# A two-block transformer kernel: gathers and weights fetched one stage ahead, one root for two norms, and new orders at the openings of four stages

## What is computed

```python
# x: 1024 tokens x 1024 columns, float32; EPS 1e-6
x = x + concat(differential_attention, latent_attention)(rms(x) @ w_in) @ w_out     # first mixer
x = x + cross_attention(rms(x), rms(mem))                                           # 256 memory rows
logits = rms(x) @ routers                       # 4 groups x 8 experts, 2 experts for each token
order = argsort(expert_ids); dest = padded_start[sorted_e] + rank   # 47 blocks of 128 slots, one expert each
y = (silu(h[tok] @ w_gate[e]) * (h[tok] @ w_up[e])) @ w_down[e]     # for each block
x = x + sum of its two rows of y, each times its routing weight
x = rms(x) * norm_final_g                       # end of the first block
h = rms(x) * attn_norm_2                        # start of the second block
proj = h @ w_in_2                               # fox, conv, mlstm and sliding-window mixers, gates
x = x + merge(...) @ w_merge_out; x = x + swiglu(rms(x))
```

## Time and profile before

| what | value |
|---|---|
| median of 3 runs (lowest, highest) | 3330.19 us (3329.55, 3349.68) |
| the profiled execution's own time | 3333.73 us |
| its span | 3332.0 us |
| its mean granted TensorE clock | 0.965 of full speed |
| PE busy, share of the span | 3121.0 us, 94% |
| PEld | 2479.6 us, 74% |
| DVE | 1697.6 us, 51% |
| ACT | 1456.4 us, 44% |
| POOL | 326.4 us, 10% |
| DMA | 413.50 MB, mean 124 GB/s |

### The profile page before, as it was taken

The page is one execution under the profiler, slowest core; times in us unless marked ns, Lnnn a source line. Parts: engine busy times, 40 slices in busy tenths (PEclk is TensorE's granted clock), DMA queues, the critical chain, the costliest instruction groups (busy, mean ns, idle before and its releaser), DMA issues. The chain is left out here.

```text
span 3332.0 us, 39537 instructions
## 1 busy us (share of the span) xinstructions
PE 3121.0 (94%) x14936; PEld 2479.6 (74%) x14936; DVE 1697.6 (51%) x2533; ACT 1456.4 (44%) x2355; POOL 326.4 (10%) x343
## 2 busy tenths in 40 slices
PE   7998999898879999969998999999989989999999
PEld 5766998776757767757776877777777868888787
DVE  4436887424655665562321222332247486666675
ACT  4325787533436666653522333333353342322343
POOL 0001110000212222120000000000000022222000
PEclk9999999999979999979999999999999999999999
DMA  2344221211157777661233222232254323334653
GB/s 96 84 127 120 58 62 40 100 74 49 77 206 273 289 289 277 225 202 45 82 97 105 64 64 76 64 108 83 79 187 160 102 79 111 95 104 131 218 151 112
DMA packets 251533, 413.50 MB, mean 124 GB/s; under 512 B 44999, under 2 KB 159758, under 8 KB 239058
## 3 DMA queue, kind: packets, MB, share of 16 engines
q1 hardware_dynamic: 226706, 365.31, 34.1%
q10 hardware_dynamic: 9088, 28.84, 2.2%
q0 software_dynamic: 15552, 16.82, 1.7%
HBM read 370.01 MB, written 104.30 MB: 142 GB/s over the span
## 5 line engine op out<-in xcount | busy, mean ns | idle before, releaser
L2753 DVE TENSOR_TENSOR moe_wgu_low<-moe_raw,moe_wgu_high 128x2048 fp32r<-128x2048 f32 x92 | 206.7, 2289 | 180.2 <-ACT moe_wgu_high L2711 180.2
L213 PE MATMUL ga_gate<-second_h_high,ga_ws_high 128*128 128x512 f32 x512 | 231.8, 453 | 0.0
L214 PE MATMUL ga_gate<-second_h_low,ga_ws_high 128*128 128x512 f32 x512 | 204.5, 399 | 0.0
L215 PE MATMUL ga_gate<-second_h_high,ga_ws_low 128*128 128x512 f32 x512 | 204.4, 399 | 0.0
L2679 PE MATMUL moe_down<-moe_raw_down,moe_ht 128*128 128x512 f32 x376 | 169.2, 593 | 1.7 <-ACT moe_ht L2743 1.7
L2711 ACT ACTIVATE moe_wgu_high<-moe_raw 128x2048 fp32r<-128x2048 f32 x92 | 170.7, 1906 | 0.0
L3730 ACT ACTIVATE ga_row<-ga_turned 128x256 f32<-128x256 f32 (+4 forms) x96 | 44.7, 465 | 275.3 <-PE ga_turned L3644 275.3
L213 PE MATMUL pr_acc<-second_h_high,pr_ws_high 128*128 128x512 f32 x352 | 147.0, 418 | 11.7 <-DVE pr_stage L3053 8.2
L213 PE MATMUL moe_up<-moe_wgu_high,moe_xt_high 128*128 128x512 f32 x376 | 152.2, 405 | 4.2 <-DVE moe_xt_low L2759 4.2
L213 PE MATMUL up_bank<-second_h_high,up_w_high 128*128 128x512 f32 x352 | 138.3, 393 | 10.8 <-DVE up_w_low L3301 7.7
L215 PE MATMUL moe_up<-moe_wgu_high,moe_xt_low 128*128 128x512 f32 x376 | 148.2, 394 | 0.0
(11 more groups left out here) (592 smaller groups left out, 7961.2 us busy)
## 6 DMA issues: line engine op xcount, KB each, us to landing
moe_raw<-in_w_expert_gate_dram SPq DMA_DIRECT2D x32, 1024.0 KB, 8.4
moe_raw<-in_w_expert_up_dram SPq DMA_DIRECT2D x32, 1024.0 KB, 10.1
moe_raw_down<-in_w_expert_down_dram SPq DMA_DIRECT2D x32, 1024.0 KB, 7.5
scratch_expert_rows<-moe_y ACTq DMA_DIRECT2D x47, 512.0 KB, 8.3
scratch_hidden<-X SPq DMA_DIRECT2D x77, 256.0 KB, 2.1
down_rows<-scratch_hidden SPq DMA_DIRECT2D x73, 256.0 KB, 2.8
ga_w<-in_w_in_dram SPq DMA_DIRECT2D x32, 512.0 KB, 4.2
scratch_gates<-ga_stage SPq DMA_DIRECT2D x64, 256.0 KB, 3.6
```

Of the source, the lines that this page charges most:

```text
L213: nc.tensor.matmul(out, w[0], x[0], start=start, stop=False)
L214: nc.tensor.matmul(out, w[0], x[1], start=False, stop=False)
L215: return nc.tensor.matmul(out, w[1], x[0], start=False, stop=stop)
L2753: nc.vector.tensor_tensor(wgu[i % 2][1][:, :, m, :], raw[(2 * i + m) % RAW][:].rearrange("p (c n) -> p c n", n=FF), wgu[i % 2][0][:, :, m, ...
```

## The change

In `first_tokens` seven raw weight buffers replace six and loads wait only for a buffer; x tile 2 goes ahead of weight chunk 7; a one-element square root (`probe`) loads the root table at the start; root and scale of tile 0 move ahead of weights; and tile 0's product is made in three passes over the chunks: high x high, then activation high x weight low, then activation low x weight high (before: three matmuls chunk by chunk). `mixed_queries` gets the same probe and three passes, and its first splits are reordered. `route` keeps counts by one scan and float32r matmuls, makes the one-hot lanes in two DVE instructions, puts the token numbers on the block side (eight ACT copies), and holds back `first_low` until POOL has issued its two gathers. At the end of `run_experts` SP fetches the next stage's first four weight chunks and the gain, the last result is copied and stored in two halves by ACT and DVE, and POOL gathers tile 0's expert rows there. In `mixer_tokens` a new step `grow` writes x * gain into the first gathered row's buffer `rows[0]`; its square gives the second norm, one root and one reciprocal serve both norms, `scale_rows` and `final_rows` read that buffer, and `final_rows(t - 1)` now comes after `add_experts(t)`, `grow(t)` and `apply_gain(t - 1)`; POOL's gathers for tile t wait for `final_rows(t - 2)` and `scale_rows(t - 2)` as well. The diff, cut to its core and moved left by eight columns:

```diff
     def load_weight(c):
-        if c >= 4:
-            sp.wait_ge(w_highs, c - 3)
-        if c >= 6:
-            sp.wait_ge(w_lows, c - 5)
-        sp.dma_start(raw[c % 6][:], w_view[:, c, COL_VD:COL_CQ]).then_inc(w_in[c % 4], 16)
+        if c >= RING:
+            sp.wait_ge(w_lows, c - RING + 1)
+        sp.dma_start(raw[c % RING][:], w_view[:, c, COL_VD:COL_CQ]).then_inc(w_in[c % RING], 16)
-    for c in range(3, KD):
+    for c in range(3, RING):
         load_weight(c)
     load_x(2)
+    for c in range(RING, KD):
+        load_weight(c)
     load_x(3)
...
+    def first_products():
+        pe.wait_ge(highs, 1)
+        for h_part, w_part in ((0, 0), (0, 1), (1, 0)):
+            if h_part:
+                pe.wait_ge(lows, 1)
+                turn_rows(2)
+            for c in range(KD):
+                if w_part:
+                    pe.wait_ge(w_lows, c + 1)
+                elif not h_part:
+                    pe.wait_ge(w_highs, c + 1)
+                last = nc.tensor.matmul(acc[0][:], H[h_part][:, c, 0:P], w[w_part][:, c, :],
+                                        start=(h_part + w_part + c == 0), stop=(h_part == 1 and c == KD - 1))
+            if h_part + w_part == 0:
+                turn_rows(1)
+        last.then_inc(products, 1)
+
...
     act.dma_start(gain_rows[0:first_count, :], gain_source("norm_mix_g")).then_inc(gain_in, 16)
+    act.wait_ge(k.chains["pool"].sem, 3)
+    nc.scalar.activation(probe[:], k.ones[:, 0:1], ACT.Sqrt)
     square(0)
     weight(0)
+    take_root(0)
+    scale_rows(0)
     weight(1)
-    take_root(0)
     weight(2)
-    scale_rows(0)
     square(1)
+    weight(3)
+    high_part(0)
     take_root(1)
     scale_rows(1)
-    high_part(0)
...
     average(0)
     weight(0)
+    inverse(0)
     weight(1)
-    inverse(0)
+    dve.wait_ge(gains_copied, 1)
+    apply_gain(0)
     weight(2)
     average(1)
+    weight(3)
     inverse(1)
-    dve.wait_ge(gains_copied, 1)
-    apply_gain(0)
     low_part(0)
...
+    def first_out_rows():
+        pe.wait_ge(highs_in, 1)
+        for in_part, w_part in ((0, 0), (0, 1), (1, 0)):
+            if in_part:
+                pe.wait_ge(lows_in, 1)
+                turn_in(1)
+            for c in range(KD):
+                if w_part:
+                    pe.wait_ge(w_lows, c + 1)
+                elif not in_part:
+                    pe.wait_ge(w_highs, c + 1)
+                for h in range(2):
+                    last = nc.tensor.matmul(acc[:, h * HALF:(h + 1) * HALF], inner[0][in_part][:, c, :],
+                                            W[w_part][:, c, h * HALF:(h + 1) * HALF],
+                                            start=(in_part + w_part + c == 0), stop=(in_part == 1 and c == KD - 1))
+        last.then_inc(products, 1)
     turn_in(0)
-    for i in range(ST + 2):
+    first_out_rows()
+    for i in range(1, ST + 2):
...
 
+    nc.scalar.activation(probe[:], k.ones[:, 0:1], ACT.Sqrt)
     squares(0)
-    weight(0)
     root(0)
     latent_scale(0)
+    weight(0)
     weight(1)
+    high_in(0)
     weight(2)
-    high_in(0)
     weight(3)
     squares(1)
+    root(1)
     weight(4)
+    latent_scale(1)
     weight(5)
-    root(1)
-    latent_scale(1)
...
     sums(0)
+    diff_scale(0)
     weight(0)
-    diff_scale(0)
     weight(1)
+    low_in(0)
     weight(2)
-    low_in(0)
+    sums(1)
     weight(3)
-    sums(1)
+    diff_scale(1)
     weight(4)
     weight(5)
-    diff_scale(1)
...
-    link(v.tensor_tensor(both[:, :, :], hot[0][:, :, :], hot[1][:, :, :], ALU.add))
-    link(v.memset(before[:, 0, :], 0.0))
-    for t in range(ST):
-        link(v.tensor_tensor(before[:, t + 1, :], before[:, t, :], both[:, t, :], ALU.add))
-    dve.sem_inc(hot_made, 1)
+    link(v.tensor_tensor(both[:, :, :].rearrange("p e t -> p t e"), hot[:, 0, :, :], hot[:, 1, :, :], ALU.add))
+    dve.wait_ge(made, 15)
+    v.tensor_tensor_scan(upto[:, :, :].rearrange("p e t -> p (e t)"), carried[:, :, :].rearrange("p e t -> p (e t)"),
+                         both[:, :, :].bitcast(F32).rearrange("p e t -> p (e t)"), 0.0, ALU.mult, ALU.add).then_inc(hot_made, 1)
...
-        link(v.tensor_tensor(hot[c][:, :, :], hot[c][:, :, :], place[:, :, :], ALU.mult))
-        link(v.tensor_reduce(slot_f[:, c * ST:(c + 1) * ST], hot[c][:, :, :], AX, ALU.add))
+    link(v.tensor_tensor(placed[:, :, :, :], hot[:, :, :, :], place[:, :, :].rearrange("p (o t) e -> p o t e", o=1)
+                         .broadcast_to([P, 2, ST, E]), ALU.mult))
+    link(v.tensor_reduce(slot_f[:].rearrange("p (c t) -> p c t", c=2), placed[:, :, :, :], AX, ALU.add))
...
+    v.tensor_tensor(hot_block[:, :, :], along(base_f[:], N_BLOCKS),
+                    bases[:, :].rearrange("p (o b) -> p o b", o=1).broadcast_to([P, 2 * ST, N_BLOCKS]),
+                    ALU.is_equal).then_inc(blocks_made, 1)
...
-    for j in range(2 * ST):
-        t = j % ST
-        v.tensor_scalar(hot_lane[j][:], lanes[:], lane_f[:, j:j + 1], tokens[:, t:t + 1],
-                        ALU.is_equal, ALU.mult).then_inc(lanes_made, 1)
+    for c in range(2):
+        v.tensor_tensor(hot_lane[:, c * ST:(c + 1) * ST, :], along(lane_f[:, c * ST:(c + 1) * ST], P),
+                        lanes[:, :].rearrange("p (o n) -> p o n", o=1).broadcast_to([P, ST, P]),
+                        ALU.is_equal).then_inc(lanes_made, 1)
...
+    dve.wait_ge(tabled, 1)
+    link(v.tensor_scalar(empty[:], table[:, 0:N_BLOCKS], 0.0, NO_TOKEN, ALU.is_equal, ALU.mult))
+    v.scalar_tensor_tensor(slot_of_block[:], table[:, 0:N_BLOCKS], -1.0, empty[:], ALU.add, ALU.add).then_inc(slotted, 1)
+    dve.wait_ge(gathers, 1)
     first_low(0)
-    dve.wait_ge(tabled, 1)
-    link(v.tensor_scalar(empty[:], table[:], 0.0, NO_TOKEN, ALU.is_equal, ALU.mult))
-    v.scalar_tensor_tensor(slot_of_block[:], table[:], -1.0, empty[:], ALU.add, ALU.add).then_inc(slotted, 1)
     first_low(1)
...
-    nc.tensor.matmul(counts[:, :], k.ones[:], before[:, ST, :], start=True, stop=True)
-    nc.tensor.matmul(ranks[:, :, :], earlier[:], both[:, :, :], start=True, stop=False)
-    nc.tensor.matmul(ranks[:, :, :], k.ones[:], before[:, 0:ST, :], start=False, stop=True).then_inc(ranked, 1)
+    nc.tensor.matmul(counts[:, :], ones_r[:], upto[:, :, ST - 1], start=True, stop=True)
+    nc.tensor.matmul(ranks[:, :, :], not_earlier_r[:], by_tile[0], start=True, stop=False)
+    nc.tensor.matmul(ranks[:, :, :], ones_r[:], by_tile[1], start=False, stop=True).then_inc(ranked, 1)
     for j in range(2 * ST):
-        pe.wait_ge(lanes_made, j + 1)
-        last = nc.tensor.matmul(table[:], hot_lane[j][:], hot_block[:, j, :], start=(j == 0),
+        pe.wait_ge(tokens_made, j % ST + 1)
+        pe.wait_ge(lanes_made, j // ST + 1)
+        last = nc.tensor.matmul(table[:], hot_lane[:, j, :], token_block[:, j, :], start=(j == 0),
...
+    gain, mixer_raw, _ = ahead
+    sp.wait_ge(ups, N - 1)
+    for c in range(1, 4):
+        load_mixer_weight(k, sp, mixer_raw[c], c)
+    sp.wait_ge(ups, N)
+    sp.dma_start(gain, k.dram["norm_final_g"].rearrange("(o d) -> o d", o=1).broadcast_to([P, D])).then_inc(k.final_gain_in, 16)
+    load_mixer_weight(k, sp, mixer_raw[0], 0)
+    sp.wait_ge(tail_copied, 1)
+    sp.dma_start(y_out[SEQUENCE[N - 1]][:, HALF:], y[(N - 1) % 2][:, HALF:]).then_inc(tail_stored, 16)
...
+    pool.wait_ge(ups, N)
+    pool.wait_ge(stored0, 16 * ((N + 1) // 2))
+    pool.wait_ge(stored1, 16 * (N // 2))
+    pool.wait_ge(tail_stored, 16)
+    for c in range(2):
+        gather_outputs(k, slots, c, 0, ahead[2][c])
...
-        nc.scalar.activation(y[i % 2][:], down[:], ACT.Copy).then_inc(y_ready, 1)
+        cols = slice(0, D if i + 1 < N else HALF)
+        nc.scalar.activation(y[i % 2][:, cols], down[:, cols], ACT.Copy).then_inc(y_ready, 1)
         act.wait_ge(y_ready, i + 1)
-        act.dma_start(y_out[SEQUENCE[i]], y[i % 2][:]).then_inc(stored[i % 2], 16)
+        act.dma_start(y_out[SEQUENCE[i]][:, cols], y[i % 2][:, cols]).then_inc(stored[i % 2], 16)
...
+    dve.wait_ge(downs, N)
+    dve.wait_ge(stored[(N - 1) % 2], 16 * ((N - 1) // 2))
+    nc.vector.tensor_copy(y[(N - 1) % 2][:, HALF:], down[:, HALF:]).then_inc(tail_copied, 1)
...
         if t >= 2:
             pool.wait_ge(added, 2 * (t - 2) + 2)
+            pool.wait_ge(normed, t - 1)
+            pool.wait_ge(scales, t - 1)
         for c in range(2):
-            nc.gpsimd.indirect_dma_start(out=rows[c][t % 2], out_offset=None, in_=k.scratch["expert_rows"],
-                                         in_offset=bass.IndirectOffsetOnAxis(ap=slots[c][:, t:t + 1], axis=0)
-                                         ).then_inc(gathered[t % 4], 16)
+            if t:
+                gather_outputs(k, slots, c, t, rows[c][t % 2])
...
-    weight(0)
-    weight(1)
+    for c in range(4):
+        weight(c)
+    nc.scalar.activation(probe[:], k.ones[:, 0:1], ACT.Sqrt)
     square(0, 0)
-    weight(2)
-    take_root(0, 0)
-    weight(3)
     square(0, 1)
-    take_root(0, 1)
+    take_roots(0)
...
```

(98 more changed lines are left out.)

159 lines of the change are left out of this document (76 added, 83 removed).

## The result

The changed kernel takes 3354.05 us (median of 12 runs, 3350.95 to 3366.46), the kernel before 3330.48 in the same session: a ratio of 1.0075, 95% interval 1.0061 to 1.0089. The forecast was 3351, range 3336 to 3364. The profiled execution took 3354.84 us with a span of 3353.0, the old one's was 3332.0: +21.0. The table puts that together from the two traces; each entry is how far the changed kernel is ahead (-) or behind (+), and how much each part added.

A forecast was written before the change was run, and what follows sets the result against it. PE was taken to bound the kernel, losing time at stage openings, until waits through a shared buffer bound `mixer_tokens`. -7 + 3 - 5.3 + 30.4 = +21 us gave 3354.8 from the profiled run, 3351 from the median; range 3336 to 3364.

The forecast's parts named there:

- First stage, -7: First stage: earlier root, high-part start and earlier tile 1 bring its transposes forward; -7.4, cut to -7 us for gaps.
- the end that I had given as -8.5: First stage: the forecast's fast end, -8.5 us, if the clock rises as soon as tile 0's second pass begins.
- Attention output stage, +3: `mixed_queries`: the late last weight chunk delays second pass, second transposes and add into x; +1.8 to +5.2, taken as +3 us.
- Routing, -5.3: Routing: slots at 927.4 instead of 933.6, first expert transposes at 937.6 instead of 942.93; -5.3 us, range -4 to -6.5.
- the wait of `first_low`: Routing: `first_low` on DVE waits for both gathers' issue, until 930, costing DVE 2.5 us.
- `mixer_tokens`, +30.4: `mixer_tokens`: waits through the gathered row's buffer make the stage end at 1552.8 instead of 1522.4, +30.4 us.
- The opening, -5: Start of `mixer_tokens`: gathers without barrier, one root and ready weights bring the first matmul to 1449.7 from 1454.56, -5 us.
- The period, 12.9: `mixer_tokens` loop: gather issue, landing and DVE's steps sum to 12.9 us per tile, where PE needs 8.5.
- the ring: `mixer_tokens`: gathers wait for `final_rows(t - 2)`, which stands behind tile t - 1's adds, which wait for gathers; 12.9 us per tile.
- That the gathers stay hidden (3316): Rival for `mixer_tokens`: POOL's added waits end before the old one, PE still bounds the loop; -14, 3316 us; 5%.
- the fast price of 2.8: Rival for `mixer_tokens`: gathers land in 2.8 us, period 10.1, stage +16, kernel 3337 us; 9%.
- PE did not become the bound: Rival for `mixer_tokens`: idle PE keeps its low clock, 14.8 us of work per tile, so PE bounds; 3367 us; 10%.

The follow-up runs named there:

- e10: The changed kernel without the probe of the square root in the first stage: 3354.11 us.
- e6: The changed kernel with tile 0 of the attention output stage multiplied chunk by chunk again, probe and split order kept: 3348.11 us (one run).
- e7: The changed kernel without DVE's wait for POOL's two gathers ahead of `first_low` in the routing: 3360.19 us (one run).
- e3: The changed kernel with tile 0's two gathers behind the barrier again, as in the kernel before: 3363.24 us, ratio 1.0102.
- e5: The changed kernel with own buffers for grown rows, first gathers behind the barrier, and POOL's four waits at the expert block's end removed: 3314.14 us, ratio 0.9949.
- e1: The changed kernel with grown rows in two idle buffers and POOL waiting for the adds alone: 3317.6 us, ratio 0.9961.

## Why the prediction came out right

By its sum it was right, by its steps only in part, and some errors cancel.

- **First stage, -7.** Measured -10.3. The start of PE, 12.8, came at 12.54; but "the root comes some 3.3 us sooner" with the probe was mostly put down to the wrong edit: the root starts at 9.76 before, 5.98 in the changed kernel and 7.34 in e10, so the probe gives 1.4 of it and the order of ACT's instructions 2.4. The mis-sized term is tile 0's end, 25.5, which came at 23.0: I kept PE slow for too many of its 24 matmuls. It was slow for the first eight and one set of transposes, 5.7 us. This is the mechanism of the end that I had given as -8.5, with more in it.
- **Attention output stage, +3.** Measured +3.5, by the chain named: last weight, second pass, second transposes, low part, add. e6 shows it. It was luck that the last weight came at nearly the same time in the two profiles, 18.5 and 18.8 us into the stage; it scatters by more than 2 us.
- **Routing, -5.3.** Measured -6.9. The slots came 6.05 sooner, 6.2 forecast. "What is late next is DVE" held, by a hair: DVE's last instruction ended at 927.38 and POOL's DRAIN, which the sum did not have, at 927.39; what DVE still had to do to leave its program (to 927.65) came last. In the kernel before and in e7 it is DRAIN. The mis-sized term is the wait of `first_low`, "930", 2.6 us after the slots: it started 1.3 after them, at 920.74, because it did not wait for both gathers' issue, only until POOL's queue had passed them, 0.35 us after the first began. That is most of the 1.6.
- **`mixer_tokens`, +30.4.** Measured +39.6. Two terms. The opening, -5, was +0.6: "the gathers need no barrier" was right and of no use, since the adds do need it, and POOL's DRAIN held it back to 1425 (e3, e5). With POOL let go, in e5, the first product comes 26.8 us after the last `moe_down`, against 29.8 before and 30.3 in the changed kernel: of the -5, 3 were there to be had. The period, 12.9, was 14.0. For the tile shown: POOL starts 0.74 after `final_rows` (0.3 forecast), the second gather follows after 2.07 (1.24), it lands 5.3 later (5.6), and DVE takes 5.7 (5.8). The 2.07 has a reason that the prediction had among its routing rows, 2.31 us beside a tensor_tensor, and left out of the ring: the first gather's issue began beside the low part and took 1.77 us, not 0.94. From the first product to the last: 12.5 to tile 2's adds (12.8), 70.2 for five periods (64.5), 24.2 behind (25.8), in all 106.9 against 103.1. These two, 5.6 and 3.8, are the 9 us.
- **The sum.** +21 was forecast and measured; the 9 us missed in `mixer_tokens` stand against 5 us missed as gains ahead of it and 4 us behind it that are no part of the change. Against the medians the forecast was 3 us low.
- **The rivals.** That the gathers stay hidden (3316) did not happen, but e1 makes it so and lands at 3317.6. No gather of the ring landed at the fast price of 2.8; the fastest took 4.4. The clock in the loop read 0.83 in the mean of 1453 to 1523, not 0.5, and PE did not become the bound.

## What to carry to other kernels

Where a buffer takes on a second use, follow its free point through the order of the engine that frees it: here one line placed behind the next tile's adds turned a transfer with a tile of slack into a ring, and placed ahead of them it cost 21 us less. Let POOL reach the end of a block early; a wait given to it there, even for work that no one else does, lays its DRAIN open. A first pass over high parts alone pays where the high parts are there (first stage, some 1.5 us), and costs where the last one is what is late (attention output stage, 4.2 us).
